# GpSimd takes the remainders of the down weights, and the experts run in an alternating order, in a hybrid encoder block with 64 experts

## The reference, cut to what matters

```python
scores = sigmoid(xf @ w_router)            # 64 experts in 8 groups
# per token: the best 4 groups, in them the best 8 experts, gates normalised to 2.5
# per expert: its tokens, padded to blocks of 128 rows
h   = silu(xb @ w_gate[e]) * (xb @ w_up[e])
out = (h @ w_down[e]) * gate[:, None]
y   = y.at[tok].add(out)
out = rms_norm(h + y + shared_expert(hn), final_norm_g)
```

## Time and profile before

| | |
|---|---|
| median of 3 runs | 1400.49 us |
| the profiled execution | 1402.79 us |
| its span, first to last instruction | 1401.1 us |
| TensorE, busy share of the span | 95% |
| VectorE | 61% |
| ScalarE | 52% |
| GpSimd | 34% |
| the 16 DMA engines, mean rate | 241 GB/s |
| granted TensorE clock, mean | 0.981 |

### The profile page before, as it was taken

How to read it: one execution, slowest core, us unless ns; L and a number is a source line. 1 busy time by engine, 2 the same in 40 slices (tenths; PEclk the granted TensorE clock), 3 DMA queues, 4 the chain that set the end, 5 groups by cost and what they waited for, 6 DMA issues and landing times.

```text
span 1401.1 us, 25069 instructions
## 1 busy us (share of the span) xinstructions
PE 1327.6 (95%) x6025; PEld 1036.9 (74%) x6026; DVE 860.0 (61%) x1186; ACT 726.3 (52%) x916; POOL 477.6 (34%) x610
## 2 busy tenths in 40 slices
PE   6999988999999999999999999999999999999995
PEld 5885465888445888888878888878877788788774
DVE  5430543446565667667866566786687756675665
ACT  5321244221011576756865557675577756665752
POOL 2431201000001345435543334453354433433462
PEclk9999998999999999999999999999999999999998
DMA  9604022102306799999998889999899998998979
GB/s 347 181 6 161 5 115 91 46 31 102 131 16 233 251 307 329 341 294 317 336 369 264 247 264 297 375 351 276 262 350 372 354 268 264 323 317 273 301 240 242
DMA packets 88306, 338.01 MB, mean 241 GB/s; under 512 B 12497, under 2 KB 23761, under 8 KB 71505
## 3 DMA queue, kind: packets, MB, share of 16 engines
q1 hardware_dynamic: 60624, 250.53, 46.0%
q0 software_dynamic: 27648, 87.06, 27.5%
HBM read 288.99 MB, written 65.27 MB: 253 GB/s over the span
## 4 chain that ended last, share of the span: by engine, by line
PE 73%; DMA 9%; ACT 6%; DVE 4%; issue 4%; ACTq 2%; DVEq 1%; SPq 0%; POOL 0%; POOLq 0%
PE ps L719 28%; PE ps_out L733 11%; PE ps L611 6%; PE ps L477 6%; DMA raw_gu<-in_w_up 5%; PE ps L460 5%; PE ps L646 4%; PE ps L513 4%; ACT w_gu L944 3%; DMA ya_in<-y_rows_dram 2%; PE ps L562 2%; ACT w_dn L948 2%; DVE xTl L1336 1%; DMA raw_dn<-in_w_down 1%; PE ps_out L628 1%
## 5 line engine op out<-in xcount | busy, mean ns | idle before, releaser
L719 PE MATMUL ps<-w_gu,xTh 128*128 x1488 | 473.2, 399 | 21.6 <-DVE xTl L1336 20.6
L1188 DVE TENSOR_TENSOR w_gu<-raw_gu,w_gu (+1 forms) x128 | 293.5, 2293 | 106.8 <-ACT w_gu L944 106.3
L719 PEld LDWEIGHTS ps<-w_gu,xTh 128*128 128x128 f32 x1488 | 276.6, 190 | 84.6 <-issue 29.3
L719 PE MATMUL ps<-w_gu,xTl 128*128 x744 | 293.6, 395 | 0.0
L944 ACT ACTIVATE w_gu<-raw_gu (+1 forms) x128 | 245.6, 1920 | 17.8 <-SPq L396 17.7
L1543 POOL DMA_INDIRECT y_rows_dram<-ob,idxs x90 | 178.0, 1978 | 201.0 <-ACT ob L965 187.1
L733 PE MATMUL ps_out<-w_dn,hTh 128*128 x744 | 242.1, 407 | 1.6 <-ACT ob L965 1.6
L1195 DVE TENSOR_TENSOR w_dn<-raw_dn,w_dn (+1 forms) x128 | 150.9, 1220 | 69.0 <-ACT w_dn L948 69.0
L719 PEld LDWEIGHTS ps<-w_gu,xTl 128*128 128x128 f32 x744 | 141.3, 190 | 29.0
L1336 DVE TENSOR_TENSOR xTl<-ps,xTh 128x512 fp32r<-128x512 f32 x186 | 119.6, 685 | 55.2 <-ACT xTh L959 55.2
L733 PEld LDWEIGHTS ps_out<-w_dn,hTh 128*128 128x128 f32 x744 | 133.2, 189 | 26.9 <-issue 1.9
(11 more groups left out here) (213 smaller groups left out, 1581.2 us busy)
## 6 DMA issues: line engine op xcount, KB each, us to landing
raw_gu<-in_w_gate SPq DMA_DIRECT2D x64, 1024.0 KB, 7.0
raw_gu<-in_w_up SPq DMA_DIRECT2D x64, 1024.0 KB, 9.8
raw_dn<-in_w_down SPq DMA_DIRECT2D x64, 1024.0 KB, 12.7
y_rows_dram<-zero SPq DMA_DIRECT2D x1, 4608.0 KB, 20.0
x_ring<-in_x SPq DMA_DIRECT2D x8, 512.0 KB, 4.6
w_in_sb<-in_w_in SPq DMA_DIRECT2D x8, 512.0 KB, 9.7
xh<-in_x SPq DMA_DIRECT2D x8, 512.0 KB, 7.1
w_out_sb<-in_w_out SPq DMA_DIRECT2D x1, 4096.0 KB, 12.8
```

Of the source, the lines that this page charges most:

```text
L719: mm = pe.matmul(ps[3][:, :], x_[:, k, :], w_gu[:, bass.ds(at, 1), part, :, k, :], start=(k == 0 and part == 0 and x_ is xTh), stop=(k == ...
L1188: dv.tensor_tensor(gu_part(w_gu[:, :, 1, :, :, :], at, m), gu_part(raw_gu, at, m), gu_part(w_gu[:, :, 0, :, :, :], at, m).bitcast(F32), AL ...
```

## The change

It has five parts. (1) A third row of `tab` holds an order of the experts in which those with two items and those with one alternate, and positions in that order take the place of the experts' numbers wherever weights are split, loaded and used. (2) The loads of the first two experts wait for the tables. (3) The marks have room for four chunks, and the shared expert's blocks and the tables stand in another order. (4) `rest_dn` moves from VectorE to GpSimd, into GpSimd's item i for the expert that begins with item i, between the gather and `add_rows`; VectorE now does both halves of `rest_gu` before `rest_h`. (5) In the tail the one-hot rows get other room and come earlier.

```diff
-        onehot = place("onehot", [P, TURN, S], F32R, Z_AT)
+        onehot = [place(f"onehot{u}", [P, S], F32R, W_AT + 32 * KB + u * GATED * 4) for u in range(TURN)]
...
-            for e in range(2):
-                load_gu(sp, e, 1 - e)
-                load_dn(sp, e, 1 - e)
-
             sp.wait_ge(s_gates, 1)
             sp.dma_start(gates_v[:, :, D:], rt_a[:, :, :]).then_inc(s_gst, 16)
+            sp.wait_ge(s_tab, 1)
+            for j in range(2):
+                e = look(sp, 2, j, NE - 1)
+                load_gu(sp, e, 1 - j)
+                load_dn(sp, e, 1 - j)
...
-                load_dn(sp, e, at)
+                load_dn(sp, look(sp, 2, j, NE - 1), at)
...
-            sp.wait_ge(s_hd, NE * KF)
-            sp.sem_inc(s_turn_sp, 1)
-            sp.wait_ge(s_ld, NE * KF)
-            sp.sem_inc(s_turn_sp, 1)
...
             pe.wait_ge(s_chunks, 1)
-            pe.matmul(ps[6][:, 0:NE], nchb[:, :], triI[:, :], start=True, stop=True).then_inc(s_pm, 1)
-            s_gate_up(1, 0)
+            pe.matmul(ps[7][:, 0:NE], nchb[:, :], upto[:, :], start=True, stop=True)
...
+            n_multi, n_single = kinds[:, 0:1], kinds[:, 1:2]
+            many((dv.tensor_scalar(n_multi, ps[6][0:NE, 2 * NE:2 * NE + 1], 1.0, None, ALU.max),
...
+            step(dv.tensor_scalar(upto[:, :], key_t[:, 0, :], kinds[:, 3:4], None, ALU.is_ge))
             dv.sem_inc(s_chunks, 1)
             shared_h(0)
...
+            shared_h(3)
             dv.wait_ge(s_table, NC)
             dv.tensor_scalar(idx_all[:, :], ps[5][:, 0:TAB], float(FAR), dump[:, 0:1], ALU.add, ALU.min).then_inc(s_idx, 1)
             dv.wait_ge(s_idx, 1)
             dv.tensor_tensor(row_all[:, :], idx_all[:, :], copy_row[:, :], ALU.add).then_inc(s_idx, 1)
-            shared_h(3)
...
                 with dv.If(ahead[0] > 0):
-                    rest_gu(ahead[2], ahead[1], (0,))
+                    rest_gu(ahead[2], ahead[1], range(GU_PARTS))
                 rest_h(i)
-                with dv.If(ahead[0] > 0):
-                    rest_gu(ahead[2], ahead[1], (1,))
-                with dv.If(coming[0] > 0):
-                    rest_dn(coming[2], coming[1])
                 return ahead
...
+            def rest_dn(i):
+
+                both = look(gp, 1, i, 2 * NE - 1)
+                e = gp.snap(both // 2, min_val=0, max_val=NE - 1)
+                at = place_of(gp, e)
+                with gp.If(gp.snap(both % 2, min_val=0, max_val=1) > 0):
+                    for k in range(KF):
+                        gp.wait_ge(s_hd, e * KF + k + 1)
+                        gp.sem_inc(s_turn, 1)
+                        gp.tensor_tensor(w_dn[:, bass.ds(at, 1), 1, k, :], raw_dn[:, bass.ds(at, 1), k, :],
+                                         w_dn[:, bass.ds(at, 1), 0, k, :].bitcast(F32), ALU.subtract).then_inc(s_ld, 1)
+
             def item(i, u, turn):
 
                 keep_gate(i + 1, (u + 1) % TURN)
                 gather(i + 1 + TURN, (u + 1) % TURN)
                 if not (isinstance(i, int) and i == 0):
+                    rest_dn(i)
+                if not (isinstance(i, int) and i == 0):
                     add_rows(i - 1, (u - 1) % TURN, turn if u else turn - 1)
```

More of the change, by code:

```diff
@@ L168, in build @@
         gidx = place("gidx", [P, NC, 8], U32, M_AT + 3 * KB + 256)
+        key_t = place("key_t", [NE, 4, NE], F32, M_AT)
+        multi = place("multi", [NE, P], BF16, M_AT + 3 * KB + 768)
         etop = place("etop", [P, NC, 8], F32, M_AT + 3 * KB + 512)
@@ L193, in build @@
         cols = place("cols", [P, 12], F32)
-        tab = place("tab", [2, TAB], I32)
+        tab = place("tab", [3, TAB], I32)
+        identb = place("identb", [NE, NE], BF16)
+        upto = place("upto", [NE, NE], BF16)
+        kinds = place("kinds", [NE, 4], F32)
+        pidx1 = place("pidx1", [P, 1], F32)
         ends = place("ends", [1, 8], I32)
@@ L780, in _ @@
             pe.wait_ge(s_hm, 4)
-            for c in range(4):
+            for c in range(5):
                 s_down(c)
             turn_item(0, 1)
-            for c in range(4, NC):
+            for c in range(5, NC):
                 s_down(c)
@@ new lines, in _ @@
+            step(dv.tensor_scalar(n_single, kinds[:, 2:3], 1.0, None, ALU.max))
+            many((dv.tensor_scalar(key_t[:, 0, :], key_t[:, 0, :], 0.5, n_multi, ALU.add, ALU.mult),
+                  dv.tensor_scalar(key_t[:, 1, :], before, n_single, None, ALU.mult)))
+            step(dv.scalar_tensor_tensor(out=key_t[:, 1, :], in0=key_t[:, 1, :], scalar=0.25, in1=key_t[:, 0, :],
+                                         op0=ALU.add, op1=ALU.subtract))
+            step(dv.tensor_tensor(key_t[:, 1, :], key_t[:, 1, :], is_multi, ALU.mult))
@@ L1348, in expert, with item @@
                 return dv.snap(both % 2, min_val=0, max_val=1), e, place_of(dv, e)
-            def item(i, u, coming, final=False):
+            def item(i, u, now, coming, final=False):
                 gated_h(i, u)
@@ L1355, in item @@
                         rest_xT(i + 1)
+                        with dv.If(now[0] > 0):
+                            dv.wait_ge(s_ld, now[1] * KF)
+                            rest_dn(now[2], now[1])
                     rest_h(i)
@@ L1365, in item @@
                 with dv.If(ahead[0] > 0):
-                    rest_gu(ahead[2], ahead[1], (0,))
+                    rest_gu(ahead[2], ahead[1], range(GU_PARTS))
                 rest_h(i)
-                with dv.If(ahead[0] > 0):
-                    rest_gu(ahead[2], ahead[1], (1,))
-                with dv.If(coming[0] > 0):
-                    rest_dn(coming[2], coming[1])
                 return ahead
             def turn_of_items(turn, final=False):
-                coming = expert(turn * TURN + 1)
+                now, coming = expert(turn * TURN), expert(turn * TURN + 1)
                 for u in range(TURN):
-                    coming = item(turn * TURN + u, u, coming, final and u > 0)
+                    now, coming = coming, item(turn * TURN + u, u, now, coming, final and u > 0)
             def y0(c):
@@ L1579, in _, with rows_of @@
             first = (two_less + 1) * TURN
+            gp.wait_ge(s_tok, 1)
+            def rows_of(u):
+                gp.tensor_copy(slot_col[:, u:u + 1], idx_all[:, bass.ds(first + u, 1)]).then_inc(s_col, 1)
+                gp.wait_ge(s_col, u + 1)
+                gp.tensor_scalar(onehot[u][:, :], tok_row[:, :], slot_col[:, u:u + 1], None, ALU.is_equal).then_inc(s_oh, 1)
             keep_gate(first + 1, 1)
+            rest_dn(first)
             add_rows(two_less * TURN + (TURN - 1), TURN - 1, two_less)
+            gathers = turns(gp)
+            gp.wait_ge(s_ga[0], gathers * 16 + 16)
+            rows_of(0)
+            rows_of(1)
             keep_gate(first + 2, 2)
[L1584 to L1593 removed]
+            rows_of(2)
             for c in range(NC):
```

96 lines of the change are left out of this document (54 added, 42 removed).

## The result

The change makes the kernel slower: 1533.65 us, the median of 4 runs (1527.2 to 1536.66), against 1400.67 beside it, a ratio of 1.0938 with a 95% interval of 1.0913 to 1.0962. The prediction had slower at 1579 within 1455 to 1655: sign and range hold, the middle is 45 us too high. The profiled execution, the fastest of the four, took 1527.2 us with a span of 1525.5 us. Ratios and medians here are of executions at the usual clock, but for one of `e3_psum`: at a mean clock of 0.75 it took 1670.85 us and is in its median (1420.59; 1419.7 without it), not in its ratio.

What follows compares the result with a forecast made beforehand. TensorE, busy 95%, was taken as the bound. Stops and clock +219, order -38 and tail -2 gave +179, so 1582 us on the profiled 1402.8; the median lies 2.3 lower, 1579 us, range 1455 to 1655.

Steps and rivals of the forecast that it cites:

- What bounds the kernel: TensorE, busy 95% of the span; time comes and goes only where it waits.
- the 866 us without waits: Stage of 92 items, first to last gate_up, at 9.41 us each; the measured 904.4 held 38 us of waits.
- Length of GpSimd's subtraction, 2.4 us: Each of GpSimd's two 128x1024 subtractions in rest_dn takes 2.4 us, between 2.2 and 2.58.
- Turn-taking: GpSimd's rest_dn and VectorE's rest_gu run one whole instruction at a time, rest_h ending 3.2 us late in 35 items.
- Rival (A): VectorE and GpSimd don't block each other; only 29 x 0.8 us through SyncE is left: 1384 us, faster; chance 0.13.
- The place of the stops: TensorE idle before down some 35 times, released by rest_h or GpSimd, and 29 times through SyncE's late landing word.
- The two together: In a two-item expert's first item, late ScalarE and GpSimd make down wait 4.0 us (3.2 to 4.4), besides 0.8.
- The clock: After each of 35 stops TensorE falls to 1.2 instead of 2.4 GHz, charged 1.45 us; lower end nothing.
- the working's +219: Stage loss before the order's -38: 29 x (0.8 + 4.0 + 1.45) = 181, plus 38 for six one-item pairs.
- With the order, both kinds of wait go, -38 us: Alternating order removes waits from both VectorE splits in successive one-item experts and from late weights: at most -38 us.
- Start and tail: First experts' loads cost nothing; marks and small products 0, within 1 us; tail -2 us, between 0 and -4.
- Rival (C): GpSimd itself becomes the bound in the items: 1623 us, or 1650 with late raw down weights; chance 0.17.

Runs made afterwards that it cites:

- e3: Changed kernel, but inside the items VectorE's rest_gu reads its first input from PSUM instead of SBUF: 1420.59 us, ratio 1.0138.
- e8: Changed kernel with the edits of e3 and e4 together (PSUM input, and SyncE's early wait for the landed down weights): 1382.8 us, ratio 0.9851.
- e4: Changed kernel, but SyncE tells that the down weights have landed before it waits to load the next ones: 1523.06 us, ratio 1.0869.
- e13: Changed kernel, with SyncE's reads of the expert's number moved ahead of its waits: 1546.04 us, ratio 1.1034.
- e6: Changed kernel, but experts in natural order and the down-weight remainders back on VectorE: 1409.6 us, ratio 1.0051.
- e10: e6 with SyncE's reads of the expert's number moved ahead of its waits: 1397.66 us, ratio 0.9974.
- e1: Changed kernel, but down-weight remainders back on VectorE and rest_h between the halves of rest_gu; alternating order kept: 1414.37 us, ratio 1.009.
- e11: e1 with SyncE's reads of the expert's number moved ahead of its waits: 1395.8 us, ratio 0.9961.

## Why the prediction was right, and where its sum was off

**What bounds the kernel: right.** In each of these kernels the 866 us without waits, TensorE's idle time and what the lower clock costs add up to the stage but for 6 to 23 us.

**Length of GpSimd's subtraction, 2.4 us: right.** 4.75 us for two when alone, 2.39 each in e3's mean. The estimate worked out from the Trainium skill (GPSIMD Engine Reference, section Performance versus the Vector engine), 2.25, is 6% short.

**Turn-taking: right, and shown.** e3 takes only VectorE's second SBUF operand away and 113 of 133 us go. Rival (A), no blocking, had 1384; its condition made true gives 1420.6, so its sum was 37 us short too: its 23 us of stops are 39, and another 20 us of the stage are neither stops nor in the 866. That e8, which adds the early wait, comes to 1382.8, near its number, is luck.

**The place of the stops: right.** Predicted were 35 stops before `down` ended by `rest_h` or GpSimd, and 29 before `gate_up`; measured 37 and 31. Of the 37 `rest_h` ends 32 and GpSimd one; 4 are under 0.3 us. (For 5 of the 32 the profile names ScalarE's `w_dn`, but that is the next expert's, which `down` doesn't wait for; `rest_h` ends 0.1 to 0.3 us before it.)

**Their size: the step that was off.** "The two together" took 4.0 us before `down` and 0.8 before `gate_up`, 35 x 4.8 = 168 us (with the clock 219). Measured are 70.9 / 37 = 1.9 and 41.4 / 31 = 1.3, 114 us with `turn_h`. My chain let ScalarE's lateness and the full turn-taking add up, both against a `down` due only 0.8 later. In the trace a late ScalarE also puts VectorE's pair behind part of GpSimd's (7.19 us, not 9), and e4 and e13 show the other side: where ScalarE or the loads are on time, the stop before `down` is longer, 2.8 and 2.3 us in the mean instead of 1.9. So the two latenesses share part of their microseconds.

**The clock: right in kind, too often.** 35 falls at 1.45 us were 51 us; the trace has 20, worth 31, so about 1.5 each: the price was right and the number was not.

**Items: missing.** From the 866 us without waits that the prediction starts from, 114 of stops and 31 of clock leave 23 us of the 1033. 16 of them stand between the transposes of the gathered rows and `down`, which wants `rest_h`: from the first transpose to the start of `down`, without the stops in the table, it is 0.98 us in the mean of 92 items and was 0.80. The profile's modelled ends of the matmuls hide this as work. The other 6 are in the kernel before as well (904.4 less 866, less 26 of stops and 6 of clock). So the working's +219 is +167 as measured: -54 for the stops, -20 for the clock, +23 that it put at nothing (rounded). That the middle is only 45 us off is in part luck: these 23 stood against 74 too many.

**"With the order, both kinds of wait go, -38 us": wrong.** The order was to spread VectorE's work. With VectorE's remainders and the reads hidden its stage is 905.2 us against 904.4. What I overlooked is that one item in three begins no expert itself but has one at i+1 and another at i+2. In e8, where GpSimd has the remainders, nothing takes turns and SyncE tells early, the stage is 13 us shorter than before: that much of the 38 is there once VectorE has less to do. In the sum the error hid in the stops, which replaced those waits; read alone, the -38 would have sent me wrong.

**Reads in SyncE's queue: not priced.** The diff shows `look` inside the load, and the working has no term for it. With VectorE's remainders it costs 12 us in the natural order (e6 to e10) and 19 in the alternating one (e1 to e11). Beside GpSimd's subtractions it costs nothing: taking it away makes 12 us more.

**Start and tail: near.** First `gate_up` 2.3 us earlier (predicted 0, within 1), tail -2.2 (predicted -2). With VectorE's remainders the same tail is 7 us shorter. Where most of the other 5 go the traces show: GpSimd fetches the summed rows back in 8 loads, and the last of them starts 20.8 us behind the last `gate_up` here, while in e11 all 8 are out 15.2 us behind it. In the final norm VectorE then waits for rows four times here (4.2 us) and once in e11 (0.7 us):

```profile
1495.51 0.87 POOL L1650 DMA_DIRECT2D ya_in<-y_rows_dram  x1 [3.51 <-DMA ya_in<-y_rows_dram]
...
1515.54 1.29 DVE L1450 TENSOR_TENSOR ya_in<-ps,ya_in 128x512 f32<-128x512 f32 x2 [1.35 <-DMA ya_in<-y_rows_dram]
```

**Rival (C), GpSimd as the bound: no.** It is busy 785 of 1033 us, and no wait of TensorE in the stage is ended by its gather or gate.

## What to carry to other kernels

Before you move a subtraction of two SBUF operands from VectorE to GpSimd, look what VectorE does at that time: if it reads two SBUF operands too, the work isn't moved but put in series, and both are longer. With one of VectorE's operands in PSUM both kept their length here. When two latenesses meet, work out the time at which the last one ends rather than add them, and look which stop grows: here the clock fell more often behind a stop of 2 us or more than behind a shorter one. And a number that is read from a table at run time belongs ahead of the waits of the queue that uses it; in a stage where DMA is busy 94% of the time, about 1 us at each load cost 12 to 19 us in all, and without it the kernels with VectorE's remainders were 3 to 5 us faster than before.

## What the runs showed of the hardware

Small GpSimd work is held up as well: the copy of one column takes 0.18 us in the rhythm before this one and 2.25 at 1176.38 in the timeline above, until VectorE's pair ends at 1178.58. A prefetch of an index thus pays for a subtraction that has nothing to do with it.

The one-hot rows, a GpSimd operation with one float16 tensor input, had seemed an exception. e10 shows that it is one in one direction only. GpSimd's row, then VectorE's:

```profile
1346.34 4.79 POOL L1637 TENSOR_SCALAR onehot<-tok_row,slot_col 128x1024 fp32r<-128x1024 f16 x1
1351.37 2.86 POOL L1637 TENSOR_SCALAR onehot<-tok_row,slot_col 128x1024 fp32r<-128x1024 f16 x1
...
1346.12 2.35 DVE L1211 TENSOR_TENSOR w_dn<-raw_dn,w_dn  x2
...
1353.14 2.36 DVE L1211 TENSOR_TENSOR w_dn<-raw_dn,w_dn  x2 [1.77 <-ACT w_dn L964]
```

The first one-hot row starts 0.2 us into VectorE's pair and takes 4.79 us, 1.93 more than the second, so it waited for about the pair's end (1348.47). VectorE's second pair starts at 1353.14 while the second row runs until 1354.23, and it isn't longer by anything. The prediction read this half only, and called it a disagreement with the rule that the Trainium skill gives (SBUF — State Buffer, section SBUF: two separate sides). That rule holds here for a running VectorE and not for a running one-hot operation.
